# W and XW products of a triangular solve interleaved on four quarters of the TensorE array, with gate products moved between them

## The reference, cut to what matters

```python
def step(S, inp):                      # one position, one head; S is 64x64
    r_t, w_t, k_t, v_t, a_t, b_t = inp
    Sa = jnp.einsum("bhvk,bhk->bhv", S, a_t)
    S = S * w_t[:, :, None, :] + Sa[..., None] * b_t[:, :, None, :] + v_t[..., None] * k_t[:, :, None, :]
    y = jnp.einsum("bhvk,bhk->bhv", S, r_t)
    return S, y
...
gate_a, gate_b = jnp.split(jax.nn.sigmoid(h @ w_gate[i] + b_gate[i]), 2, axis=-1)
merged = gate_a * (y_a @ w_branch_a[i]) + gate_b * (y_b @ w_branch_b[i])
```

## Time and profile before

| | |
|---|---|
| median of 3 runs | 969.11 us (968.95 to 969.68) |
| the profiled execution's own time | 969.92 us |
| its span, first to last instruction | 968.1 us |
| PE busy | 946.6 us (98%), 6759 matmuls |
| DVE, ACT, POOL busy | 400.6, 421.2, 384.9 us |
| mean granted TensorE clock | 0.997 |
| the solve, 291.90 to 340.18 us | 48.28 us |
| the recurrence over chunks, 340.18 to 378.16 us | 37.98 us |

### The profile page before, as it was taken

The page is one execution under the profiler, slowest core; times in us unless marked ns, Lnnn a source line. Parts: engine busy times, 40 slices in busy tenths (PEclk is TensorE's granted clock), DMA queues, the critical chain, the costliest instruction groups (busy, mean ns, idle before and its releaser), DMA issues.

```text
span 968.1 us, 15831 instructions
## 1 busy us (share of the span) xinstructions
PE 946.6 (98%) x6759; PEld 787.8 (81%) x6759; DVE 400.6 (41%) x634; ACT 421.2 (44%) x665; POOL 384.9 (40%) x180
## 2 busy tenths in 40 slices
PE   6999999999999999999999999999999999999996
PEld 4887888887779988888788888888888888888885
DVE  4224798217645465058343434344433400100435
ACT  6355553236555244424435443444434421422646
POOL 2442444332216142435613444344444444345350
PEclk9999999999999999999999999999999999999998
DMA  8432433331211000325512333333333242333232
GB/s 252 121 102 63 98 87 87 93 104 45 65 46 26 4 3 2 109 72 185 158 39 69 88 109 88 107 89 100 97 92 104 88 130 87 97 99 112 66 106 88
DMA packets 115163, 86.59 MB, mean 89 GB/s; under 512 B 2852, under 2 KB 100022, under 8 KB 115094
## 3 DMA queue, kind: packets, MB, share of 16 engines
q1 hardware_dynamic: 114904, 85.50, 30.2%
q10 hardware_dynamic: 190, 0.08, 0.0%
HBM read 83.47 MB, written 2.10 MB: 88 GB/s over the span
## 4 chain that ended last, share of the span: by engine, by line
PE 94%; DVE 2%; ACT 1%; issue 1%; POOL 1%; DMA 1%; SPq 0%; DVEq 0%; ACTq 0%
PE bank L540 18%; PE bank L541 18%; PE bank L542 18%; PE bank L584 9%; PE bank L585 9%; PE bank L586 9%; PE bank L825 2%; PE bank L835 2%; PE bank L707 1%; PE bank L744 1%; PE bank L721 1%; DMA xs<-in_x_dram 1%; PE bank L792 1%; PE bank L803 1%; POOL w_lo L520 0%
## 5 line engine op out<-in xcount | busy, mean ns | idle before, releaser
L520 POOL TENSOR_TENSOR w_lo<-raw,w_hi 128x1024 fp32r<-128x1024 f32 x138 | 332.7, 2411 | 506.1 <-ACT w_hi L1078 506.0
L1078 ACT ACTIVATE w_hi<-raw 128x1024 fp32r<-128x1024 f32 x138 | 146.5, 1061 | 357.3 <-issue 217.2
L540 PE MATMUL bank<-hT_hi,w_hi 128*128 128x512 f32 (+1 forms) x736 | 285.6, 388 | 1.0 <-POOL w_lo L520 0.9
L541 PE MATMUL bank<-hT_lo,w_hi 128*128 128x512 f32 (+1 forms) x736 | 283.0, 385 | 0.0
L542 PE MATMUL bank<-hT_hi,w_lo 128*128 128x512 f32 (+1 forms) x736 | 283.0, 385 | 0.0
L540 PEld LDWEIGHTS bank<-hT_hi,w_hi 128*128 128x128 f32 x736 | 138.2, 188 | 29.5 <-issue 1.4
L542 PEld LDWEIGHTS bank<-hT_hi,w_lo 128*128 128x128 f32 x736 | 138.2, 188 | 27.6
L541 PEld LDWEIGHTS bank<-hT_lo,w_hi 128*128 128x128 f32 x736 | 138.3, 188 | 26.6
L1944 DVE SCALAR_TENSOR_TENSOR cbuf<-bank,params,cbuf 128x511 f32<-128x511 f32 x48 | 36.0, 750 | 134.0 <-ACT cbuf L1456 134.0
L584 PE MATMUL bank<-w_hi,g_hi 128*128 128x512 f32 x184 | 71.7, 389 | 0.0
L586 PE MATMUL bank<-w_hi,g_lo 128*128 128x512 f32 x184 | 71.6, 389 | 0.0
(11 more groups left out here) (290 smaller groups left out, 1284.7 us busy)
## 6 DMA issues: line engine op xcount, KB each, us to landing
raw<-in_w_up_dram SPq DMA_DIRECT2D x48, 512.0 KB, 3.8
raw<-in_w_in_dram SPq DMA_DIRECT2D x33, 512.0 KB, 4.0
raw<-in_w_down_dram SPq DMA_DIRECT2D x24, 512.0 KB, 3.8
raw<-in_w_gate_dram SPq DMA_DIRECT2D x16, 512.0 KB, 3.9
raw<-in_w_out_dram SPq DMA_DIRECT2D x8, 512.0 KB, 4.4
raw<-in_w_ple_gate_dram SPq DMA_DIRECT2D x8, 512.0 KB, 4.6
xs<-in_x_dram SPq DMA_DIRECT2D x4, 512.0 KB, 5.4
raw<-in_w_branch_a_dram SPq DMA_DIRECT2D x4, 512.0 KB, 3.5
```

The costliest lines, as they stand in the source:

```text
L520: nc.gpsimd.tensor_tensor(low(n)[:, :], raw[:, n % RAW_SLOTS, :], high(n)[:, :].bitcast(F32), ALU.subtract).then_inc(*step("pool", ("lo", n)))
L540: nc.tensor.matmul(o, wh, ah, start=first, stop=False)
L541: nc.tensor.matmul(o, wh, al, start=False, stop=False)
L1078: nc.scalar.activation(high(u)[:, :], raw[:, u % RAW_SLOTS, :], ACT.Copy) \
```

## The change

1. **Solve.** `level_both(g, lv, h, lw)` issues group h's XW of level lw and group g's W of level lv product by product in turn. W's output goes to the other half of the partitions (`half(1 - q)`), so that a W product sits in the quarter beside the XW product's, and the four products of one turn sit in the four quarters. ACT copies W out in two instructions, each half to the other half. 18 calls of W and 18 of XW are joined so; two of W (groups 0 and 1, level 0) and two of XW (groups 2 and 3, level 4) stay alone.
2. **Gates.** After every second joined call of levels 1 to 4 comes one gate part, eight in all: unit `GATE_ORDER[8]` is made within the solve, in bank 7, which the solve's ring no longer uses. ACT copies it out as `raw_gate` after the first chunk (`gate_of_solve`), followed by the high part of a later unit, and applies the sigmoid later. Chunks 5, 6 and 7 get one gate part more each.
3. **RA.** b against r (64 moving columns) and keys against r and a (128) are separate products with 64x64 stationary operands, spread over four quarters; b against a, which nothing used, is gone.
4. **`with_state`.** The products into u1 and into y are issued in turn, y in the other two quarters; y's halves are swapped from there on.
5. **Order over chunks.** `own_values(c + 1)` is issued whole, ahead of `solved_u(c)`; transpositions and gate parts of chunks 6 and 7 move ahead of `own_values`; RA(c + 3) comes after `solved_u(c)`, for c below 5, and RA(2) moves into the solve's beginning.
6. **Copies.** DVE takes one head of u, keys and values of every chunk or group from 1 on; ACT takes all of RA's.

```diff
-        ring, given, holder = {"any": RING}, {r: 0 for r in (RING, CHUNK_RING, STEP_RING, GATE_RING, Y_RING, FILL_RING, U_RING, Z_RING, SIXTH,
+        SOLVE_RING = range(7)
+        ring, given, holder = {"any": RING}, {r: 0 for r in (RING, SOLVE_RING, CHUNK_RING, STEP_RING, GATE_RING, Y_RING, FILL_RING, U_RING, Z_RING, SIXTH,
...
             def with_r_and_a(c):
                 o = [begin("RA", c, q) for q in range(2)]
                 for p in range(NPAIR):
+                    keys = [Kb[half(q), p, c, 1, :] for q in range(2)]
+                    bs = [Kb[half(q), p, c, 0, :] for q in range(2)]
                     for q in range(2):
-                        view = o[q][:, :].rearrange("p (two h t) -> p two h t", two=2, h=NPAIR)
-                        mm = nc.tensor.matmul(view[:, :, p, :], keys_and_b(p, q, c), RA[half(q), :, p, chunk_cols(c)],
+                        nc.tensor.matmul(o[q][half(0), p * CH:(p + 1) * CH], bs[q], Rr[half(q), p, chunk_cols(c)],
+                                         start=True, stop=True)
+                        view = o[1 - q][half(1), :].rearrange("p (two h t) -> p two h t", two=2, h=NPAIR)
+                        mm = nc.tensor.matmul(view[:, :, p, :], keys[1 - q], RA[half(1 - q), :, p, chunk_cols(c)],
                                               start=True, stop=True)
...
+            def product_w(o, g, lv, n, q):
+                x = right_columns(Xs[:, g, :, :, :].rearrange("p s h t -> p (s h) t"), 2 << lv)
+                w = o[half(1 - q), n * 32:(n + 1) * 32].rearrange("p (k b) -> p k b", b=2 << lv)
+                return nc.tensor.matmul(w, Am[half(q), g, n // NPAIR, n % NPAIR, :], x[half(q), n, :, :], start=True, stop=True)
+
+            def product_xw(o, g, n, q):
+                return nc.tensor.matmul(o[half(q), n * 32:(n + 1) * 32], XT[half(q), g, n // NPAIR, n % NPAIR, :],
+                                        Wp[half(q), g, n, :], start=True, stop=True)
...
+            def level_both(g, lv, h, lw):
+
+                u, o = begin_xw(h, lw), begin_w(g, lv)
+                for n in range(2 * NPAIR):
+                    for q in range(2):
+                        of_xw = product_xw(u, h, n, q)
+                        of_w = product_w(o, g, lv, n, q)
+                of_xw.then_inc(*step("pe", ("XW", h, lw)))
+                of_w.then_inc(*step("pe", ("W", g, lv)))
...
                 for p in range(NPAIR):
                     for q in range(2):
                         mm = nc.tensor.matmul(held["u1"][half(q), cols], KK[half(q), p, chunk_cols(c)],
                                               Zs[half(q), c % 2, p, :], start=False, stop=True, skip_group_check=True)
-                mm.then_inc(*step("pe", ("u1", c)))
-                for p in range(NPAIR):
-                    for q in range(2):
-                        nc.tensor.matmul(y[half(q), p * CH:(p + 1) * CH], Rr[half(q), p, chunk_cols(c)],
+                        if p == NPAIR - 1 and q:
+                            mm.then_inc(*step("pe", ("u1", c)))
+                        nc.tensor.matmul(y[half(1 - q), cols], Rr[half(q), p, chunk_cols(c)],
                                          Zs[half(q), c % 2, p, :], start=p == 0, stop=False, skip_group_check=True)
...
-            level_w(2, 0)
+            level_both(2, 0, 0, 0)
             tokens_of_values(0)
-            level_w(3, 0)
-            for lv in range(5):
-                if lv:
-                    for g in range(4):
-                        level_w(g, lv)
-                if lv in (1, 2):
-                    with_r_and_a(lv + 1)
-                for g in range(4):
-                    level_xw(g, lv)
+            level_both(3, 0, 1, 0)
+            with_r_and_a(2)
+            for lv in range(1, 5):
+                level_both(0, lv, 2, lv - 1)
+                level_both(1, lv, 3, lv - 1)
+                gate_parts(1)
+                level_both(2, lv, 0, lv)
+                level_both(3, lv, 1, lv)
+                gate_parts(1)
+            level_xw(2, 4)
+            level_xw(3, 4)
+            ring.clear()
...
             for c in range(NCH):
                 with_state(c)
                 if c == 0:
                     tokens_of_values(1)
-                if c in (2, 3, 4):
-                    with_r_and_a(c + 3)
-                solved_u(c)
-                if c + 1 < NCH:
-                    own_values(c + 1, range(NPAIR // 2))
-                if c == 0:
-                    tokens_of_keys(1)
                 if c == 1:
-                    with_r_and_a(4)
+                    tokens_of_keys(1)
...
+                if c + 1 < NCH:
+                    own_values(c + 1)
+                solved_u(c)
+                if c < 5:
+                    with_r_and_a(c + 3)
+                else:
+                    gate_parts(1)
                 state_and_output(c)
...
-            gate_parts(KD - 2)
-            for i in GATE_ORDER[9:14]:
+            gate_parts(KD - 5)
+            for i in GATE_ORDER[10:14]:
...
+            def gate_of_solve(i):
+                act.wait_ge(*done("pe", "gate", i))
+                nc.scalar.activation(raw_gate[:, :], psum(("gate", i))[:, :], ACT.Identity,
+                                     bias=par("b_gate", i)).then_inc(*frees("act", ("gate", i), ("graw", i)))
+                before(("gate", i))
...
-                nc.scalar.activation(Wp[:, g, :, :].rearrange("p n t -> p (n t)"), psum(("W", g, lv))[:, 0:256], ACT.Copy) \
-                    .then_inc(*frees("act", ("W", g, lv), ("Wp", g, lv)))
+                for q in range(2):
+                    nc.scalar.activation(Wp[half(q), g, :, :].rearrange("p n t -> p (n t)"), psum(("W", g, lv))[half(1 - q), 0:256],
+                                         ACT.Copy).then_inc(*frees("act", ("W", g, lv), ("Wp", g, lv)))
...
             for c in range(NCH):
                 if c == 0:
-                    second_half_of_values(1)
-                if c in (2, 3, 4):
-                    second_half_with_r_and_a(c + 3)
+                    second_head_of_values(1)
+                if c == 1:
+                    second_head_of_keys(1)
+                if c in (2, 4):
+                    second_head_of_values(c // 2 + 1)
+                if c in (3, 5):
+                    second_head_of_keys((c + 1) // 2)
+                second_head_of_u(c)
                 carried(c)
                 centred(c)
                 squared(c)
```

More of the change, by code:

```diff
@@ L781, in product_a @@
                               lambda s, p, q: Kb[half(q), p, 2 * g + s, 0, :]).then_inc(*step("pe", ("A", g)))
-            def keys_and_b(p, q, c):
-                return Kb[half(q), p, c, :, :].rearrange("p two t -> p (two t)")
             def with_r_and_a(c):
@@ L827, in level_w @@
                 mm.then_inc(*step("pe", ("W", g, lv)))
             def level_xw(g, lv):
-                pe.wait_ge(*done("dve", "XT", g, lv))
-                pe.wait_ge(*done("act", "Wp", g, lv))
-                o = begin("XW", g, lv)
+                o = begin_xw(g, lv)
                 for n in range(2 * NPAIR):
                     for q in range(2):
-                        mm = nc.tensor.matmul(o[half(q), n * 32:(n + 1) * 32], XT[half(q), g, n // NPAIR, n % NPAIR, :],
-                                              Wp[half(q), g, n, :], start=True, stop=True)
+                        mm = product_xw(o, g, n, q)
@@ L850, in own_values @@
+            held = {}
+            def own_values(c):
+                pe.wait_ge(*done("pool", "mask", c))
+                if c % 2 == 0:
+                    pe.wait_ge(*done("act", "Vt", c // 2))
+                    if c:
+                        pe.wait_ge(*done("dve", "Vt", c // 2))
+                held["u1"] = o = begin("u1", c)
                 v = VU[c // 2 % 2]
-                for p in pairs:
+                for p in range(NPAIR):
                     for q in range(2):
@@ L855, in own_values @@
                                               skip_group_check=True)
-                if NPAIR - 1 in pairs:
-                    mm.then_inc(*step("pe", ("own", c), *([] if c else [("u1", c)])))
+                mm.then_inc(*step("pe", ("own", c), *([] if c else [("u1", c)])))
             def with_state(c):
@@ L897, in state_and_output @@
                     mm.then_inc(*step("pe", ("z", c)))
-                    own_values(c + 1, range(NPAIR // 2, NPAIR))
                 for p in range(NPAIR):
                     for q in range(2):
-                        mm = nc.tensor.matmul(held["y"][half(q), p * CH:(p + 1) * CH], D0[:, c % 4, q, p, :],
+                        mm = nc.tensor.matmul(held["y"][half(1 - q), p * CH:(p + 1) * CH], D0[:, c % 4, q, p, :],
                                               vu[:, c % 2, q, p, :], start=not c and p == 0, stop=True,
@@ L921, in _ @@
             ring.clear()
-            ring.update(any=RING)
+            ring.update(any=SOLVE_RING, gate=ATT_OUT)
             for g in range(4):
@@ L975, in _ @@
```

(9 more changed lines are left out.)

81 lines of the change are left out of this document (38 added, 43 removed).

## The result

The changed kernel takes **975.42 us** (median of 4 runs, 974.88 to 977.51) against 969.28 for the kernel before beside it: ratio 1.0063, 95% interval 1.0049 to 1.0078. It is 0.6% slower, not 15 us faster. The profiled execution took 975.12 us, its span is 973.3.

What follows compares the result with a forecast made beforehand. It took PE, 94% of the chain, as the bound. Solve -9.9, chunks +1.6, after them -7.5 and +0.3 sum to -15.5, giving 953.6 us from the median 969.11; 8 in 10 range 949.5 to 961.5.

Steps and rivals of the forecast that it cites:

- The price of four quarters: Small products on PE: four quarters start one per 14.6 ns, needing an instruction packet every 1.9 us, which fits.
- (a): Solve: two joined calls take 0.93 us in place of 1.87, 18 times: -16.8 us.
- Rival 3: Supply or order within the queue holds the pace near 20 ns per product: 960 us, chance 0.13.
- (j): Chunks: y of chunk 1 waits for bank 7 until ACT copies out the solve's gate unit: +1.5 us.
- (k): Chunks: z waits for DVE's head of u, DVE's circle outlasting PE's work: 4 chunks x 0.85, +3.4 us.
- (f): Chunks: u1 and y in four quarters take 0.47 us for 0.93, seven times: -3.2 us.
- (b): Solve: three RA calls in the new form, 0.88 us each, save 0.33 each: -1.0 us.
- (g): Chunks: five RA calls in the new form: -1.6 us.
- (c): Solve: eight gate parts among small products, 1.01 us each with the change of shape: +8.1 us.
- (d): Solve: gate parts cover joined calls' waits for operands; only RA's copies at the beginning make ACT late: +0.4 us.
- (n): After the chunks: eleven gate parts fewer at 0.68 us each: -7.5 us.
- Rival 2: Four quarters don't work at once, as weights of one row half load one after the other: 976 us, chance 0.08.

Runs made afterwards that it cites:

- experiment 4: Changed kernel with the solve's first product group made three times over: six of ten executions 965.2 to 966.8 us, four 974.2 to 978.7.
- 5: Changed kernel with the three products of each gate part spread over the two joined calls of a half level: 964.20 us.
- 7: Changed kernel, joined calls apart, TensorE made to wait once for GpSimd: one operation 964.85 us; two operations 989.0 to 989.4 three times, 966.83 once.
- experiment 1: Changed kernel with each joined call taken apart into XW, then W: 965.41 us.
- experiment 9, first kernel: Changed kernel, solve calls apart, raw gate copied out before the chunks, order and copies of the kernel before in the chunks: 965.34 us.
- experiment 2: Changed kernel with joined calls apart and W's products back in the two quarters XW uses: 970.20 us.
- 8: Changed kernel with a gate part behind every joined call; then level 0 apart; then five chunk parts added; then all calls apart: 966.24, 966.21, 962.48, 970.99 us.
- 9: Four kernels on apart, joined or spread solves, changing the chunks' order, raw gate copy or DVE's squares: 965.34, 957.71, 971.57, 961.05 us.
- 6: Changed kernel with the solve's eight gate parts made ahead of its first product: 973.14 us.

## Why the prediction was wrong

**The step that failed** is one sentence of "The price of four quarters": "four quarters need one every 1.9 us. That fits, with less room." I took the transfer of a packet, 1.2 us, for the time between two packets. It is one of three terms: from one resumption to the next the changed kernel needs 3.40 to 4.08 us whatever it has to do in between, experiment 4 needs 3.6 to 4.1, because PE resumes only 1.2 to 1.6 us after the packet's end and the next packet starts only 1.0 to 1.4 us after that (once 1.7). The 3.7 us per packet of before were thus not a rate with half its room left; they were near the limit. The trace of before has no standstill and could not show by how much, but it gave no right to 1.9.

Forecast and result differ by 21.8 us; the stretches hold 20.8 of it:

- **(a), supply, +8.8.** The solve at full clock is 47.2 (experiment 4 without its extra products) against the forecast 38.4, and its standstills hold 9.4 us. So (a) was right for the array (0.93 us for a joined call that no standstill cuts) and wrong for what feeds it. Rival 3 had the mechanism, with a pace of 20 ns; it was 26.7, and worse.
- **The clock, +8.3 in the solve and +2.5 in the chunks.** 55.49 against 47.2, and 43.10 against 40.62; the solve's share is a difference of two kernels whose packets lie differently. No step of mine had it. At half clock a half level takes 5.15 us (two joined calls 3.35, the part 1.8), and the clock stays down for 41 us. Shown: the same products spread (5) or shifted (4) keep the clock in most executions and are then 9 to 11 us faster; with one forced idle stretch of 1.32 us it is lost in three of four (7). That the standstills of supply are what lost it in the changed kernel is argued from these three and from the place, 0.7 us behind the one of 1.36 us; what makes one standstill lose it and another not is open.
- **The chunks at full clock, +1.2.** (j) is right: +1.5 forecast, 1.16 from start to start here, 1.56 in experiment 1. (k) had the right engine but the wrong wait, and that its 3.4 us come out is luck: z doesn't wait for DVE's head of u; RA waits for the bank behind the second head of values and keys, 1.06 to 1.20 us from start to start, three times. It isn't DVE's load that costs this but its order, since moving the squares gives all of it back. (f) brought 0.2 of its 3.2 in the old order (experiment 9, first kernel), where waits for DVE's copy of RA took its place.
- **(b), (g), right.** RA takes 0.85 us from its first start to the next call's, 0.88 was priced. **(c)** right at full clock: 1.04 us from the last start before a part to the first behind it (experiment 1), 1.01 forecast.
- **(d)** small as forecast: in the solve no joined call of the changed kernel waits for a copy of W, and one of experiment 4 waits 0.66 us for ACT's copy of the transposed keys. **(n), (o), right:** 24.47 against 24.5.
- **Missed on the other side:** the calls of the new order overlap at their ends even when they aren't joined, 4.8 us of the whole (experiment 2). I had the evidence, line 853 starting before the last two of line 882, and used it only to argue for 14.6 ns.

Rival 2 (no four at once, 976 us) has nearly the measured time and is false: starts 7 ns apart show it. A time alone would have confirmed it. (Its terms as printed give 5.8 for the chunks, not 5.3, which changes nothing.) The changed kernel also speaks against the rule of the Trainium skill, "TensorE: Matmul & The Clock Gate", Part 3, that weight loads overlap only across row groups: XW and W of the same q share the row group, and their weight loads (135 ns each) and products still start 7 ns apart. The Trainium skill, "TensorEngine Tiling (Array Packing)", "Instruction Overhead", has a floor of about 60 cycles per matmul; as a floor across quarters it is refuted by 14.6 ns per product, and one quarter, with a product every 58 ns, doesn't test it. On supply, the Trainium skill, "Runtime: NRT & Kernel Launch", "Instruction fetch mechanics", says that instructions come in blocks of 256 and that the fetch is hidden because dispatch is slower. The block of 256 is what the trace shows; that the fetch is hidden is refuted here where PE takes 256 instructions in less than 3.4 to 4.1 us.

Open: what sets the length of a packet's transfer (0.88 to 1.38 us in the two solves) and the two times around it; and what decides whether the clock falls. In some kernels the clock fell in one execution and held in another (experiments 4, 5, 7, 8, 9); in the changed kernel it fell in each.

## What to carry to other kernels

Before packing small products, count instructions, not only array time: here TensorE got 256 of them (128 products with their weights) per 3.4 to 4.1 us, and products under some 27 to 32 ns each must stand among large ones, spread so that every packet has its share. Put neighbouring calls into different quarters before you interleave them: it gave 4.8 us for one swapped index. Keep idle stretches of TensorE out of a stretch of small products: behind one of 1.3 us the clock fell, and it cost 22 us. And in a circle of engines look at the order of the one that copies: moving 1.3 us of squares behind a copy gave 4 us.

## What the hardware showed that I had not expected

- TensorE stands still at every 256th of its instructions when they go faster than one packet per 3.4 to 4.1 us, up to 1.55 us idle; the releaser column shows "issue". It resumes 1.2 to 1.6 us after the packet's end, and only 1.0 to 1.4 us later, once 1.7, does the next one start.
- Four quarters take four products in 58 ns, of 32 or of 64 columns, the starts 7 ns apart, also where two of them share rows or columns. Products of a later call start ahead of the last of the call before, when their quarter is free.
- The granted clock fell to half within or up to 2 us behind idle stretches of 1.3 to 1.9 us in the midst of small products (changed kernel, experiments 6, 7, 8, 9), and held after others of 1.3 and 1.4 us. In the five kernels that lost it in or ahead of the solve's levels it stayed there for 38 to 61 us, with PE shown as busy throughout or nearly so, and came back only within the chunks. In the changed kernel that cost 11 us, with the calls apart 22 us: joined calls run at 26.2 ns a product at half clock, close to what the supply allows anyway.
